# Head normalisation of retention and mLSTM moved into their own block, with the mLSTM pairs first and their division left out

## What is computed

```python
def head_norm(x):
    mu = jnp.mean(xf, axis=-1, keepdims=True)
    var = jnp.mean(jnp.square(xf - mu), axis=-1, keepdims=True)
    return ((xf - mu) * lax.rsqrt(var + LN_EPS)).astype(x.dtype)
...
# in mlstm_chunkwise: one denominator for each token and head
    h = num / jnp.maximum(jnp.abs(den), jnp.exp(-m_q))[..., None]
...
# in token_mixers
    y_r = retention_chunkwise(...)
    o_b = (head_norm(y_r).reshape(bsz, seq, MIX_RET) * jax.nn.silu(rg)).astype(h.dtype)
    h_tilde = mlstm_chunkwise(...)
    h_t = jax.nn.sigmoid(heads(mo, N_HEADS_MLSTM).astype(jnp.float32)) * h_tilde
    o_c = head_norm(h_t).reshape(bsz, seq, MIX_MLSTM).astype(h.dtype)
    return jnp.concatenate([o_a, o_b, o_c], axis=-1) @ w_out
```

## Time and profile before

| | us |
|---|---|
| median of 3 runs | 3402.19 |
| lowest, highest | 3397.21, 3410.13 |
| the profiled execution | 3397.93 |
| its span in the trace | 3396.3 |
| its mean granted TensorE clock | 0.894 |

### The profile page before, as it was taken

The page is one execution under the profiler, slowest core; times in us unless marked ns, Lnnn a source line. Parts: engine busy times, 40 slices in busy tenths (PEclk is TensorE's granted clock), DMA queues, the critical chain, the costliest instruction groups (busy, mean ns, idle before and its releaser), DMA issues. The chain is left out here.

```text
span 3396.3 us, 41718 instructions
## 1 busy us (share of the span) xinstructions
PE 2831.7 (83%) x14724; PEld 2088.3 (61%) x14724; DVE 1682.9 (50%) x3025; ACT 938.6 (28%) x1465; POOL 748.2 (22%) x353
## 2 busy tenths in 40 slices
PE   4996775994996865996787988989999787789997
PEld 3674354332775444332677677878888574678886
DVE  5896653234697664234561765373636315341113
ACT  3224422213223523111412733112122323132122
POOL 1430010110441010110131022232334210044443
PEclk9987886996997876998898998999999888699999
DMA  6530015963541013982351011241324210022322
GB/s 243 197 125 32 1 37 236 341 240 118 173 172 46 1 37 128 348 323 98 114 209 69 1 48 64 75 161 56 127 101 150 75 71 1 13 99 93 105 89 72
DMA packets 92343, 398.20 MB, mean 117 GB/s; under 512 B 16384, under 2 KB 17952, under 8 KB 70816
## 3 DMA queue, kind: packets, MB, share of 16 engines
q1 hardware_dynamic: 63248, 303.42, 24.8%
q0 software_dynamic: 28800, 92.30, 7.5%
q10 hardware_dynamic: 144, 0.52, 0.0%
HBM read 490.04 MB, written 23.59 MB: 151 GB/s over the span
## 5 line engine op out<-in xcount | busy, mean ns | idle before, releaser
L2307 DVE TENSOR_TENSOR ffn_silu<-ffn_silu,PS 128x512 f32<-128x512 f32 x66 | 37.6, 597 | 414.8 <-ACT ffn_silu L2289 414.8
L375 POOL TENSOR_TENSOR 22_w_part<-weights_raw,22_w_part 128x2048 fp32r<-128x2048 f32 (+2 forms) x44 | 146.7, 3335 | 406.2 <-ACT 22_w_part L337 406.2
L2049 PE MATMUL PS<-one_weights_more,13_h_tokens 128*64 128x512 f32 (+1 forms) x1024 | 230.9, 603 | 2.6 <-ACT 13_h_tokens L2101 1.7
L223 PE MATMUL PS<-ffn_h_parts,22_w_part 128*128 128x512 f32 (+1 forms) x640 | 203.7, 339 | 8.6 <-DVE ffn_out_t L1543 7.8
L224 PE MATMUL PS<-ffn_h_parts,22_w_part 128*128 128x512 f32 (+1 forms) x640 | 202.7, 339 | 0.0
L375 POOL TENSOR_TENSOR 36_w_part<-weights_raw,36_w_part 128x2048 fp32r<-128x2048 f32 (+2 forms) x36 | 149.1, 4142 | 212.9 <-ACT 36_w_part L337 212.9
L375 POOL TENSOR_TENSOR 3_w_part<-weights_raw,3_w_part 128x1024 fp32r<-128x1024 f32 (+1 forms) x52 | 143.1, 2753 | 149.0 <-ACT 3_w_part L337 148.5
L2049 PEld LDWEIGHTS PS<-one_weights_more,13_h_tokens 128*64 128x64 f32 x1024 | 78.4, 139 | 132.8 <-issue 126.8
L223 PE MATMUL PS<-one_mix_h_parts,3_w_part 128*128 128x512 f32 x352 | 146.5, 416 | 0.2
L2289 ACT ACTIVATE ffn_silu<-PS 128x512 f32<-128x512 f32 x66 | 32.4, 526 | 404.5 <-PE PS L228 378.4
L224 PE MATMUL PS<-one_mix_h_parts,3_w_part 128*128 128x512 f32 x352 | 140.1, 398 | 0.0
(11 more groups left out here) (625 smaller groups left out, 7011.1 us busy)
## 6 DMA issues: line engine op xcount, KB each, us to landing
one_weights_more<-in_w_gu SPq DMA_DIRECT2D x128, 1024.0 KB, 9.1
one_weights_more<-in_w_down SPq DMA_DIRECT2D x64, 1024.0 KB, 8.4
weights_raw<-in_f_gu SPq DMA_DIRECT2D x44, 1024.0 KB, 4.8
one_values<-in_w_ada POOLq DMA_DIRECT2D x32, 1024.0 KB, 5.3
weights_raw<-in_w_proj SPq DMA_DIRECT2D x60, 512.0 KB, 3.3
ffn_shared<-in_w_ada POOLq DMA_DIRECT2D x24, 1024.0 KB, 7.0
weights_raw<-in_w_ada SPq DMA_DIRECT2D x32, 512.0 KB, 9.3
two_ab_mod_w<-in_w_ada POOLq DMA_DIRECT2D x16, 1024.0 KB, 5.2
```

The costliest lines, as they stand in the source:

```text
L223: nc.tensor.matmul(out, w[0], x[1], start=(j == 0), stop=False)
L375: self.nc.gpsimd.tensor_tensor(self.part[:, u, 1], self.raw[:, u], self.part[:, u, 0].bitcast(F32), ALU.subtract).then_inc(self.count["spl ...
L2049: mm = nc.tensor.matmul(M.PS[rows(h), 2 + i % 2, :], h_[:, i % 2, k, rows(h)], weights(i, h, k * 2 * FE), start=(k == 0), stop=(k == KD - 1))
L2307: ins = nc.vector.tensor_tensor(sl[:, u, off:off + nt], sl[:, u, off:off + nt], M.PS[:, 4 * u + 2 + a, 0:nt], ALU.mult)
```

## The change

`head_norm` as a block is gone; its instructions are issued inside `linear_mixers`, chunk by chunk, between the pairs. The chunks run in the order 2, 3, 0, 1 (mLSTM first). `divide` is gone. For an mLSTM chunk `gated` makes max(-den, floor) and then max with den (that is n), and z = numerator times gate; ACT squares n with eps in the scale, and DVE adds eps n² to the variance (`add_floor`) before ACT's root. PE's mean and variance matmuls write into banks 4 and 5, where the denominators were. Each engine's list says behind which pair a step stands.

```diff
-    s = take(M, "s_done p_done pv_done e_done y_done step")
+    s = take(M, "s_done p_done pv_done e_done z_done y_done mean cen sq var sd norm done step")
+    CHUNKS = (2, 3, 0, 1)
...
+            def mean(j):
+                pe.wait_ge(s["z_done"], j + 1)
+                if j >= 2:
+                    pe.wait_ge(s["sd"], j - 1)
+                nc.tensor.matmul(norm_bank(j), heads, B.Y[:, CHUNKS[j], :], start=True, stop=True).then_inc(s["mean"], 1)
+            def var(j):
+                pe.wait_ge(s["sq"], j + 1)
+                nc.tensor.matmul(norm_bank(j), heads, eb[:, j, :], start=True, stop=True).then_inc(s["var"], 1)
...
+            for p in range(PAIRS):
+                if p + 1 < PAIRS:
+                    scores(p + 1)
+                values(p)
+                if p in (5, 9, 12):
+                    mean((5, 9, 12).index(p))
+                if p in (7, 11, 14):
+                    var((7, 11, 14).index(p))
+            mean(3)
+            var(3)
...
-            def divide(g):
-                dve.wait_ge(s["pv_done"], TT * (g + 1))
-                step(nc.vector.tensor_scalar(den[:], M.PS[:, 4 + g % 2, :], -1.0, None, ALU.mult))
-                step(nc.vector.tensor_tensor(den[:], M.PS[:, 4 + g % 2, :], den[:], ALU.max))
-                step(nc.vector.tensor_tensor(den[:], den[:], B.floor[:, g - 2, :], ALU.max))
-                step(nc.vector.reciprocal(den[:], den[:]))
-                step(nc.vector.tensor_tensor(den[:], den[:], B.PT[:, C_MO + g - 2, :], ALU.mult))
-                nc.vector.tensor_tensor(B.Y[:, g, :], M.PS[:, 2 + g % 2, :], den[:], ALU.mult).then_inc(s["y_done"], 1)
+            def gated(j):
+                dve.wait_ge(s["pv_done"], TT * (j + 1))
+                step(nc.vector.scalar_tensor_tensor(out=den[:, j, :], in0=M.PS[:, 4 + j, :], scalar=-1.0,
+                                                    in1=B.floor[:, j, :], op0=ALU.mult, op1=ALU.max))
+                nc.vector.tensor_tensor(den[:, j, :], M.PS[:, 4 + j, :], den[:, j, :], ALU.max).then_inc(s["y_done"], 1)
+                nc.vector.tensor_tensor(B.Y[:, 2 + j, :], M.PS[:, 2 + j, :], B.PT[:, C_MO + j, :],
+                                        ALU.mult).then_inc(s["z_done"], 1)
...
+            for p in range(PAIRS):
+                weigh(2 * p)
+                weigh(2 * p + 1)
+                if p in (5, 9):
+                    gated(p // TT - 1)
+                if p in (7, 11, 14):
+                    centre((7, 11, 14).index(p))
+                if p in (9, 13):
+                    add_floor((9, 13).index(p))
+                if p == 10:
+                    norm(0)
+            norm(1)
+            centre(3)
+            norm(2)
+            norm(3)
...
-            for m in range(4):
+            for m in range(half):
                 exponent(m)
-            for g in range(2):
-                act.wait_ge(s["pv_done"], TT * (g + 1))
-                nc.scalar.activation(B.Y[:, g, :], M.PS[:, 2 + g, :], ACT.Copy).then_inc(s["y_done"], 1)
-            for m in range(4, half):
-                exponent(m)
+            squares(0)
+            roots(0)
+            squares(1)
+            copy(2)
+            roots(1)
+            squares(2)
+            roots(2)
+            copy(3)
+            squares(3)
+            roots(3)
...
-                head_norm(nc, M, B)
```

More of the change, by code:

```diff
@@ L1029, in weigh @@
                 if kind:
-                    m = n - half
-                    dve.wait_ge(s["e_done"], m + 1)
-                    step(nc.vector.scalar_tensor_tensor(out=pb[:, n % 4, 0:w], in0=eb[:, m % 4, 0:w], scalar=1.0,
+                    dve.wait_ge(s["e_done"], n + 1)
+                    step(nc.vector.scalar_tensor_tensor(out=pb[:, n % 4, 0:w], in0=eb[:, n % 4, 0:w], scalar=1.0,
                                                         in1=M.PS[:, score_bank(n), 0:w], op0=ALU.min, op1=ALU.mult))
@@ new lines, in centre, with add_floor, norm @@
+            def centre(j):
+                dve.wait_ge(s["mean"], j + 1)
+                y = B.Y[:, CHUNKS[j], :]
+                nc.vector.tensor_tensor(y, y, norm_bank(j), ALU.subtract).then_inc(s["cen"], 1)
+            def add_floor(j):
+                dve.wait_ge(s["var"], j + 1)
+                nc.vector.tensor_tensor(den[:, j, :], norm_bank(j), den[:, j, :], ALU.add).then_inc(s["sd"], 1)
+            def norm(j):
+                g = CHUNKS[j]
+                y, r = B.Y[:, g, :], den[:, j, :] if j < 2 else eb[:, j, :]
+                dve.wait_ge(s["norm"], j + 1)
+                step(nc.vector.reciprocal(r, r))
+                if g >= 2:
+                    nc.vector.tensor_tensor(B.mixT[:, 4 + g, :], y, r, ALU.mult).then_inc(s["done"], 1)
+                else:
+                    step(nc.vector.tensor_tensor(y, y, r, ALU.mult))
+                    nc.vector.tensor_tensor(B.mixT[:, 4 + g, :], y, B.PT[:, C_RG + g, :], ALU.mult).then_inc(s["done"], 1)
@@ L1068, in _ @@
-            for g in range(2):
-                act.wait_ge(s["pv_done"], TT * (g + 1))
-                nc.scalar.activation(B.Y[:, g, :], M.PS[:, 2 + g, :], ACT.Copy).then_inc(s["y_done"], 1)
-            for m in range(4, half):
-                exponent(m)
[L1073 to L1105, removed]
-                    nc.vector.tensor_tensor(B.mixT[:, 4 + c, :], cen[:, c, :], B.PT[:, C_RG + c, :],
-                                            ALU.mult).then_inc(s["done"], 1)
-        @block.scalar
-        def _(act):
-            for c in range(4):
-                act.wait_ge(s["cen"], c + 1)
-                nc.scalar.activation(sq[:, c, :], cen[:, c, :], ACT.Square).then_inc(s["sq"], 1)
-            for c in range(4):
-                act.wait_ge(s["var"], c + 1)
-                nc.scalar.activation(sq[:, c, :], M.PS[:, 4 + c, :], ACT.Sqrt, bias=M.eps[:, 0:1]).then_inc(s["sd"], 1)
@@ new lines, in squares, with roots @@
+            def squares(j):
+                if j < 2:
+                    act.wait_ge(s["y_done"], j + 1)
+                    nc.scalar.activation(den[:, j, :], den[:, j, :], ACT.Square, scale=EPS ** 0.5)
+                act.wait_ge(s["cen"], j + 1)
+                nc.scalar.activation(eb[:, j, :], B.Y[:, CHUNKS[j], :], ACT.Square).then_inc(s["sq"], 1)
+            def roots(j):
+                if j < 2:
+                    act.wait_ge(s["sd"], j + 1)
+                    nc.scalar.activation(den[:, j, :], den[:, j, :], ACT.Sqrt).then_inc(s["norm"], 1)
+                else:
+                    act.wait_ge(s["var"], j + 1)
+                    nc.scalar.activation(eb[:, j, :], norm_bank(j), ACT.Sqrt, bias=M.eps[:, 0:1]).then_inc(s["norm"], 1)
```

33 lines of the change are left out of this document (16 added, 17 removed).

## The result

| | before | after |
|---|---|---|
| first session, median | 3399.70 (4 runs, 3394.45 to 3410.13) | 3361.88 (4 runs, 3339.85 to 3375.10) |
| second session, median | 3400.41 (11 runs, 3390.74 to 3411.07) | 3356.52 (6 runs, 3343.97 to 3372.08) |
| the profiled execution | 3397.93 | 3339.85 |
| its span, its mean granted clock | 3396.3, 0.894 | 3338.2, 0.907 |

The ratio is 0.9898 in the first session, 95% interval 0.9862 to 0.9934, and 0.9868 (0.9842 to 0.9895) in the second. The forecast was 3362.6 us.

What follows compares the result with a forecast made beforehand. DVE or the chain between engines was taken to bound the step; loop 39.3, tail 14.0 and barrier 0.95 gave 54.3 us a pass against 74.05, 39.6 less for two layers: 3402.2 to 3362.6 us, range 3350 to 3379.

Steps and rivals of the forecast that it cites:

- The step is alone, and what it saves is saved: Both passes: no loads or transfers in flight, so a shorter step moves all that follows forward by as much.
- Rival 5: Behind the step: the gain is given back because what follows waits for something else; half back 3382 us; chance 0.05.
- DVE's tail, 14.0 us and a barrier of 0.95: Behind the loop: last mLSTM norm, one subtraction and two retention norms take 14.0 us where there were 36.6.
- the spare 2.3 us: Tail: the last root is done 6.9 us after the last weights, its RECIPROCAL due only after 9.2.
- The loop, 39.3 us: Pair loop: 38.4 us with 2.2 of 10.9 us added DVE work hidden, plus 0.9 for 3.4 us of half clock.
- the walk: Stepping through three engine lists with the trace's durations; for the old loop 37.0 us against 36.5 traced.
- The saving, 39.6 us: Both layers: a pass of 54.3 us against 74.05, 19.8 less each.
- Rival 2: From the first chunk's norm to the block's end the clock stays low: 13.2 us saved a pass, 3376 us; chance 0.12.
- Rival 1: In the loop the clock stays full: 0.9 us less a pass, 3361 us; within the forecast group's chance of 0.76.
- Rival 6: In the loop nothing hides, PE falls behind by 2.2 us more a pass: 3367 us; within the group's chance of 0.76.
- Rival 3: Whole block: the clock never rises, 78 us a pass against 74, 3411 us; chance 0.02.
- rival 4: ACT's roots: tables switched at every root, seven more loads of 1.3 us, 3381 us at most; chance 0.02.

Runs made afterwards that it cites:

- after_again: The changed kernel run again unchanged: 3356.52 us, ratio 0.9868, passes 56.74 and 56.77 us.
- before: The kernel before the change, as first profiled: 3397.93 us, passes 74.07 and 74.05 us.
- fill_again: Second run of the changed kernel with three unneeded matmuls in PE's list ahead of pair 11's values: 3337.53 us, passes 56.65 and 54.24 us.
- merge_only: The changed kernel, its chunk order included, with the division kept (RECIPROCAL and one more multiply in `gated`): 3376.53 us, ratio 0.9932.
- before_again: The kernel before the change run again unchanged: 3397.25 us, passes 74.03 and 73.99 us.
- defer_only: The kernel before the change, two blocks and old order, with only the division left out: 3360.78 us, ratio 0.9926.
- halves: The changed kernel with the first norm's RECIPROCAL cut into two halves, behind pairs 10 and 12: 3336.02 us, then 3353.73 us in a second run.
- start_filled: The changed kernel with the first norm's RECIPROCAL cut in two and a 256-column matmul added ahead of pair 0's values: 3334.79 us, ratio 0.9819.

## Why the prediction held, point by point

- *The step is alone, and what it saves is saved.* Right. The second pass began 24.8 us earlier than before; 17.3 of that is the first pass and the rest was won or lost outside. `after_again` and `before` both had the long stretch, and their spans differ by 33.5 us where their passes differ by 34.6. Rival 5 didn't show.
- *DVE's tail, 14.0 us and a barrier of 0.95.* From the last weights at 405.30 to 420.30 it is 15.0 us. Right to a tenth, with the spare 2.3 us measured as 2.1.
- *The loop, 39.3 us.* It measured 41.7. This is the term that was mis-sized, and by two steps. The clock fell as said, beside the norm of the first chunk, but it stayed at 0.50 for nearly 7 us (395 to 401.5) in all four passes of this kernel, not 3.4, and the 0.9 us that I gave it are 2.5 in `fill_again`. I took the length from one case, at 491. PE's work behind the gap had a break of its own here, 0.56 us, and none at 491, but no break is needed for the long form: in `merge_only` the clock stayed down for 6.7 us while PE worked without one. Why it is one length or the other stays open. The rest, 0.8 us, is the walk itself: it had 38.4 for a loop at full clock, with 0.5 taken off because it had been too long for the kernel before, and with the clock held at 1.00 `fill_again` has 39.2 (1133.50 to 1172.74). Of the 10.9 us added on DVE 1.3 were hidden then, not 2.2.
- *The saving, 39.6 us.* 34.6 by the passes, 37.8 and 43.9 by the medians. The median of 3361.88 lies 0.7 us from the forecast, and that closeness is luck: the forecast started from 3402.2, and with the passes alone it would have been 3402.2 - 34.6 = 3367.6, 5 us higher.
- *Rival 2, half clock to the end of the block.* In between: the clock came back, but after twice the time. Rival 1 (no fall) is out. Rival 6 (nothing hides) named 3367 us, which is what the passes say, but by the wrong cause: of the 2.4 us by which a pass was longer than forecast, 1.6 were the clock. Rival 3 (never up) and rival 4 (tables) didn't happen; ACT had one load a pass, in the gap where it waits 4.44 us.
- *The Trainium skill's price of a table switch* (ScalarE: Activation LUTs, What ACT_TABLE_LOAD costs) made no difference, as was said, since the gap covers either price; no run here shows the drain that the page adds.
- *What I did not see at all* is that the start of a pass can have its own lottery, worth 2.4 us, and that the rest of the program has one of 20 us; 3361.88 and the 3367.6 of the passes alone both lie inside the range.

## What stays open

Why the clock sometimes comes up only at 7.5 to 9 us. In the versions with mLSTM first and an unfilled start this was so in 6 of 18 passes, in those with retention first in none of 6, in those with the filled start in none of 4. That would fit the 0.75 us gap, but chance alone could do it with so few; the first passes of `before_again` and `defer_only`, with retention first and without that gap, still had the clock up only at 5.5 us; and the order of the chunks was not tried by itself: with retention first, the roots would stand between exponentials and each switch would load a table.

How long the clock stays down once it falls. Behind one and the same gap of 3.7 us in `merge_only` it was 6.7 us in one pass and 3.5 us in the other, and no run here says why.

Whether a version beats the changed kernel in the program's time. `halves` and `start_filled` had medians of 3336 to 3354 and 3335 us against 3357 to 3362, and their passes are 4.7 us shorter, 9.4 us for both layers. The pass is shown; the rest of the difference in the medians is the spread.

## What to carry to other kernels

When one engine's list gets a long instruction in a loop that two engines share, count what the other engine does meanwhile: 3.4 us of RECIPROCAL with its multiply cost 2.5 us of clock, and even with the clock held the pass was only 0.4 us shorter than with this norm behind the loop (54.24 and 54.68); in two pieces at places with waits of DVE it was 2.6 us shorter (52.05). A blind walk of the lists with measured durations gave the pass to 2.4 us in 56.7, and two thirds of the error were in the one thing it had a single row for, how long the clock stays down. And when a program has a spread of 20 us, judge a change of 10 by the stretch that it changes.

## What the runs showed of the hardware

- Behind PE's gap of 2.58 us the granted clock was at 0.50 from 395 to 401.5, and for as long in the other three passes of the changed kernel; three matmuls in the gap kept it at 1.00, and the pass got 2.5 us shorter by 2.84 us of added work.
- Behind one and the same gap of 3.7 us, with unbroken work after it, the clock was down for 6.7 us in one pass of `merge_only` and for 3.5 us in the other. In the first of these passes it also fell once, at 408.8, behind two gaps of 0.84 and 0.82 us with 0.44 us of work between them; in `halves` gaps of 0.38 and 0.82 us at the same place of the list left it at 1.00.
- One and the same stretch of 586 matmuls takes 119 or 137 us in two executions of one kernel, at a mean granted clock of 0.88 or 0.74.
- A RECIPROCAL of 256 columns takes 1.74 to 1.75 us, one of 512 takes 3.35, so cutting it costs 0.1 to 0.2 us of busy time.
- GpSimd multiplies 128x512 from and to SBUF in 1.29 us, and a RECIPROCAL on DVE beside it takes 3.35 us as ever.
